# Grouped columns scaled and rotated one operation to a slot; gate tiles one to a block of the output projection

## What is computed

```
for l in range(2):
    sh_a, sc_a, g_a, sh_f, sc_f, g_f = split(silu(cond) @ w_ada[l] + b_ada[l], 6)   # 6 x 1024, for two cond
    z = modulate(x, norm_mix_g, sh_a, sc_a) @ w_in[l]      # 1824 columns: MLA, neighbourhood and grouped-query parts
    gq, gk = rms_norm(gq, q_g), rms_norm(gk, k_g)          # per head of 64, grouped-query columns
    o_gqa = attention(rope(gq), [rope(gk), cache], ...)    # latents rotated; 6 query heads, 2 key heads
    x += g_a * (concat(o_mla, o_na, o_gqa) @ w_out[l])     # 16 heads in all
    x += g_f * swiglu(modulate(x, norm_ffn_g, sh_f, sc_f)) # d_ff = 2816
```

## Time and profile before

| | us |
|---|---|
| median of 3 runs | 1801.14 |
| lowest and highest | 1798.12, 1805.73 |
| the profiled execution, its own time | 1804.04 |
| its span from first to last instruction | 1802.2 |
| PE busy in the span | 1708.5 |
| DVE, ACT, POOL busy | 1139.3, 691.9, 230.8 |

### The profile page before, as it was taken

How to read it: one execution, slowest core, us unless ns; L and a number is a source line. 1 busy time by engine, 2 the same in 40 slices (tenths; PEclk the granted TensorE clock), 3 DMA queues, 4 the chain that set the end, 5 groups by cost and what they waited for, 6 DMA issues and landing times.

```text
span 1802.2 us, 28539 instructions
## 1 busy us (share of the span) xinstructions
PE 1708.5 (95%) x11410; PEld 1636.7 (91%) x11410; DVE 1139.3 (63%) x2194; ACT 691.9 (38%) x1365; POOL 230.8 (13%) x318
## 2 busy tenths in 40 slices
PE   6998889989999999999999988988999999999997
PEld 2998778888999999999999977877999999999997
DVE  5997777848867766777562576785464444444443
ACT  3536657743422222222153476675352222222222
POOL 0134452300000000000011362331000000000001
PEclk8999999999999999999999999999999999999998
DMA  9552000045333333334132000003122222222201
GB/s 357 200 196 63 1 1 2 24 156 189 135 129 128 128 117 128 128 128 145 34 91 93 17 28 1 1 1 117 47 73 92 91 71 70 70 70 70 70 24 59
DMA packets 103206, 159.79 MB, mean 89 GB/s; under 512 B 4880, under 2 KB 81488, under 8 KB 102224
## 3 DMA queue, kind: packets, MB, share of 16 engines
q1 hardware_dynamic: 101632, 155.88, 25.6%
q0 software_dynamic: 480, 2.19, 0.4%
q10 hardware_dynamic: 1008, 0.61, 0.1%
HBM read 155.09 MB, written 3.57 MB: 88 GB/s over the span
## 4 chain that ended last, share of the span: by engine, by line
PE 84%; DVE 7%; ACT 3%; DMA 2%; issue 2%; POOL 1%; SPq 1%; POOLq 0%; DVEq 0%; ACTq 0%
PE ps L660 25%; PE ps L662 25%; PE ps L661 24%; PE ps L921 3%; PE ps L891 1%; DMA wo_raw<-in_w_out 1%; DVE ps L1410 1%; PE ps L893 1%; PE ps L668 1%; PE ps L740 1%; DMA ada_n<-in_w_ada_first 1%; DVE hT L1395 1%; DVE negmax L1646 1%; PE ps L796 1%; ACT probs L1196 1%
## 5 line engine op out<-in xcount | busy, mean ns | idle before, releaser
L660 PE MATMUL ps<-hT,gw 128*128 128x320 f32 x1408 | 435.2, 309 | 2.1 <-DVE hT L1395 2.1
L662 PE MATMUL ps<-hT,gw 128*128 128x320 f32 x1408 | 435.1, 309 | 0.0
L661 PE MATMUL ps<-hT,gw 128*128 128x320 f32 x1408 | 435.1, 309 | 0.0
L1478 DVE SCALAR_TENSOR_TENSOR x<-ps,mod,x 128x320 f32<-128x320 f32 (+2 forms) x576 | 211.8, 433 | 94.2 <-PE ps L662 91.1
L660 PEld LDWEIGHTS ps<-hT,gw 128*128 128x128 f32 x1408 | 264.4, 188 | 2.9 <-issue 2.9
L661 PEld LDWEIGHTS ps<-hT,gw 128*128 128x128 f32 x1408 | 264.4, 188 | 0.0
L662 PEld LDWEIGHTS ps<-hT,gw 128*128 128x128 f32 x1408 | 264.4, 188 | 0.0
L1728 DVE TENSOR_TENSOR mm<-sl,ps 128x320 f32<-128x320 f32 x88 | 42.7, 488 | 316.7 <-issue 185.3
L660 PE MATMUL ps<-act,dw 128*128 128x320 f32 x704 | 218.3, 310 | 2.7 <-DVE act L1395 2.7
L661 PE MATMUL ps<-act,dw 128*128 128x320 f32 x704 | 218.3, 310 | 0.0
L662 PE MATMUL ps<-act,dw 128*128 128x320 f32 x704 | 218.2, 310 | 0.0
(11 more groups left out here) (226 smaller groups left out, 3545.4 us busy)
## 6 DMA issues: line engine op xcount, KB each, us to landing
gw_raw<-in_w_gate SPq DMA_DIRECT2D x22, 1024.0 KB, 5.4
gw_raw<-in_w_up SPq DMA_DIRECT2D x22, 1024.0 KB, 8.0
dw_raw<-in_w_down SPq DMA_DIRECT2D x22, 1024.0 KB, 4.9
ada_w<-in_w_adaT SPq DMA_DIRECT2D x43, 512.0 KB, 5.7
ada_wf<-in_w_adaT SPq DMA_DIRECT2D x34, 512.0 KB, 7.0
wi_raw<-in_w_in SPq DMA_DIRECT2D x12, 1216.0 KB, 6.7
wo_raw<-in_w_out SPq DMA_DIRECT2D x16, 512.0 KB, 5.0
ada_n<-in_w_ada_first SPq DMA_DIRECT2D x5, 1024.0 KB, 15.6
```

The lines of the kernel that those rows point to most:

```text
L660: pe.matmul(dst, lh, rh, start=start, stop=False, skip_group_check=True)
L661: pe.matmul(dst, lh, rl, start=False, stop=False, skip_group_check=True)
L662: return pe.matmul(dst, ll, rh, start=False, stop=stop, skip_group_check=True)
L1478: i = ve.scalar_tensor_tensor(out=x[:, o, c0:c1], in0=ps[:, banks + hf_, s0:s0 + c1 - c0], scalar=mod[:, l, part * KD + o, q:q + 1], in1=x ...
```

## The change

It has three parts.

- **Grouped columns.** An entry ("GZ", t) becomes ("G1", t), the division, in slot 25 + 2t, ("G2", t), the gains, in slot 26 + 2t, both before the slot's transposition, and ("GR", t, j), the four POOL operations of the rotation, j = 0 to 3, in slots 28 + 4t + j. So tile 3's rotation is in slots 40 to 43, in both layers. The reciprocal of all tiles' roots (1581) stays with tile 0's division.
- **Gate tiles.** `GATE_AT` goes. Block 1 computes tile 40 ahead of its residual and tile 41 behind it, blocks 2 to 7 one tile each. ACT makes `silu_f` in block 1 instead of block 2. SP issues `silu_f` and tiles 40, 41 right at the end of attention and the first feed-forward weights only after `wo_raw[3]`, in both layers; then tiles 42 and 43, and one tile per block.
- **Layer 1's tiles in layer 0's feed-forward.** Block 0 computes its four behind its residuals, none ahead of the gated products. Other blocks stay.

```diff
-GATE_AT = [0, 0, 0, 0, 2, 4, 6, 7, 8]
...
-    spread([("GZ", t) for t in range(NT)], 25, 18)
+    for t in range(NT):
+        extra[2 * (25 + 2 * t)].append(("G1", t))
+        extra[2 * (26 + 2 * t)].append(("G2", t))
+    for t in range(4):
+        for j in range(4):
+            extra[2 * (28 + 4 * t + j)].append(("GR", t, j))
...
                     if o == 1:
 
                         sp.wait_ge(o_ready, l * 2 * NP + 2 * NP)
-                        sp.dma_start(gw_raw[:, 0], a["w_gate"][l, :, 0:256].rearrange("(k p) n -> p k n", p=P)).then_inc(gw_in, 16)
-                        sp.dma_start(gw_raw[:, 1], a["w_up"][l, :, 0:256].rearrange("(k p) n -> p k n", p=P)).then_inc(gw_in, 16)
-                        sp.dma_start(dw_raw[:], a["w_down"][l, 0:256, :].rearrange("(j p) n -> p j n", p=P)).then_inc(dw_in, 16)
                         if l + 1 < DEPTH:
...
-                    if l == 0 and o >= 2:
-                        for t in GATE[2:][GATE_AT[o - 1]:GATE_AT[o]]:
+                    if o == 3:
+                        sp.dma_start(gw_raw[:, 0], a["w_gate"][l, :, 0:256].rearrange("(k p) n -> p k n", p=P)).then_inc(gw_in, 16)
+                        sp.dma_start(gw_raw[:, 1], a["w_up"][l, :, 0:256].rearrange("(k p) n -> p k n", p=P)).then_inc(gw_in, 16)
+                        sp.dma_start(dw_raw[:], a["w_down"][l, 0:256, :].rearrange("(j p) n -> p j n", p=P)).then_inc(dw_in, 16)
+                    if l == 0 and o >= 3:
+                        for t in GATE[2:4] if o == 3 else GATE[o:o + 1]:
                             ada_load(l, t)
...
-                    if o == 2 and l + 1 < DEPTH:
+                    if o == 1 and l + 1 < DEPTH:
                         sc.wait_ge(cond_in, 32)
                         sc.activation(silu_f[:], silu_f[:], ACT.Silu).then_inc(silu_done, 1)
...
                     lo(wo[:, o % 2, 1], wo_raw[:, o % 2], wo[:, o % 2, 0]).then_inc(wo_ready, 1)
+                    if o == 1 and l == 0:
+                        ve.wait_ge(silu_done, 2)
+                        ada(l, GATE[0])
                     if o >= 1:
                         residual(l, l * XD + o, o - 1, 2 + 2 * ((o - 1) % 3), 2)
                     if o >= 4:
                         add_square(l, o - 3)
-                    if l == 0:
-                        if o == 3:
-                            ve.wait_ge(silu_done, 2)
-                        for t in GATE[GATE_AT[o]:GATE_AT[o + 1]]:
-                            ada(l, t)
+                    if o >= 1 and l == 0:
+                        ada(l, GATE[o])
...
-                        for t in ahead[2 * j:2 * j + 2]:
+                        for t in ahead[2 * j:2 * j + 2] if b else ():
                             ada(l + 1, t)
...
-                    for t in ahead[4:]:
+                    for t in ahead[4:] if b else ahead:
                         ada(l + 1, t)
```

More of the change, by code:

```diff
@@ L608, in _ @@
                 for s in SCHED:
-                    if s[0] == "GZ" and s[1] == NT - 1:
+                    if s == ("G2", NT - 1):
                         sp.wait_ge(g_norm, l * NT + NT)
@@ L1337, in _ @@
                         square(2 * l + 1, l * XD + 2, o - 3)
-                    if o == 2 and l + 1 < DEPTH:
+                    if o == 1 and l + 1 < DEPTH:
                         sc.wait_ge(cond_in, 32)
                         sc.activation(silu_f[:], silu_f[:], ACT.Silu).then_inc(silu_done, 1)
-                        sc.activation(warm[:, 0:1], eps[:], ACT.Sqrt)
+                        sc.activation(warm[:, 1:2], eps[:], ACT.Sqrt)
                 def gw_split(b, j):
@@ L1577, in g_scale, with g_divide @@
                 def g_scale(t):
+                    g_divide(t)
+                    g_gain(t)
+                def g_divide(t):
                     zg = z[:, t, OFF_G:G_V].rearrange("p (h d) -> p h d", h=8)
@@ L1678, in _ @@
                         i.then_inc(v_ready, 1)
-                    elif s[0] == "GZ" and l == 0:
-                        g_scale(s[1])
+                    elif s[0] == "G1" and l == 0:
+                        g_divide(s[1])
+                    elif s[0] == "G2" and l == 0:
+                        g_gain(s[1])
                 for o in range(KD):
@@ L1768, in _, with rotate_step @@
         def _(po):
-            def rotate(own, n, d, view, cos, sin, tmp):
+            def rotate_step(j, own, n, d, view, cos, sin, tmp):
                 w = d // 4
@@ L1774, in rotate @@
                 t4 = tmp.rearrange("p h (a b w) -> p h a b w", a=2, b=2)
-                for b in range(2):
-                    po.tensor_tensor(t4[:, :, :, b, :], halves[:, :, :, 1 - b, :],
-                                     s4[:, :, b, :].unsqueeze(1).broadcast_to([P, n, 2, w]), ALU.mult).then_inc(pool_own, 1)
-                po.wait_ge(pool_own, own + 2)
-                po.tensor_tensor(view, view, cos.unsqueeze(1).broadcast_to([P, n, d]), ALU.mult).then_inc(pool_own, 1)
+                if j < 2:
+                    return po.tensor_tensor(t4[:, :, :, j, :], halves[:, :, :, 1 - j, :],
+                                            s4[:, :, j, :].unsqueeze(1).broadcast_to([P, n, 2, w]), ALU.mult).then_inc(pool_own, 1)
+                if j == 2:
+                    po.wait_ge(pool_own, own + 2)
+                    return po.tensor_tensor(view, view, cos.unsqueeze(1).broadcast_to([P, n, d]), ALU.mult).then_inc(pool_own, 1)
                 po.wait_ge(pool_own, own + 3)
                 return po.tensor_tensor(view, view, tmp, ALU.add)
+            def rotate(*turn):
+                for j in range(4):
+                    i = rotate_step(j, *turn)
+                return i
             OWN = 3 * 12
@@ L1872, in _ @@
                         value_zeros(1)
-                    elif s[0] == "GZ" and (0 if l == 0 else LATE_G) <= s[1] < 4:
-                        g_rotate(s[1], ztmp[:])
+                    elif s[0] == "GR" and s[1] >= (0 if l == 0 else LATE_G):
+                        _, t, j = s
+                        if j == 0:
+                            po.wait_ge(g_norm, l * NT + t + 1)
+                            if t:
+                                po.wait_ge(g_roped, l * 4 + t)
+                        i = rotate_step(j, *g_turn(t, ztmp[:]))
+                        if j == 3:
+                            i.then_inc(g_roped, 1)
                 add_squares(l)
```

8 lines of the change are left out of this document (5 added, 3 removed).

## The result

The changed kernel takes 1788.88 us, the median of 9 runs (1787.45 to 1792.11), beside 1801.14 us for the kernel before (9 runs of the same comparison, 1794.8 to 1807.47): a ratio of 0.9938, 95% interval 0.9918 to 0.9958. The profiled execution took 1788.93 us with a span of 1787.1, against 1804.04 and 1802.2 before. In a second comparison the two gave 1788.26 (10 runs) and 1801.25 us (33 runs), ratio 0.9949, interval 0.9931 to 0.9968. The ratios are estimates of their own: the medians alone, divided, give 0.9932 and 0.9928.

What follows compares the result with a forecast made beforehand. PE was taken to bound the kernel nearly everywhere. Gains of 4.0 + 3.6 + 4.4 = 12.0 us take the profiled execution from 1804.0 to 1792 and the median from 1801.14 to 1789, range 1784 to 1796.

Steps and rivals of the forecast that it cites:

- Grouped columns, 4.0 predicted: Layer 0's attention, slots 25 to 47: 7.5 us lost before, 3.5 after, a gain of 4.0, bounds 5.9 and -1.8.
- the cost after: Attention, slots 25 to 47: 1.6 us lost on DVE plus 1.9 at the port, 3.5 in all.
- Its first item: Slot 25: reciprocal and division on DVE, 1.1 us, with no idle to cover them, 1.0 lost.
- The item for slots 28 to 34: DVE's gains and six further operations exceed its idle: 0.35 us lost in slot 28, 0.2 in slots 29 to 34.
- rival (b): Everything hidden: DVE's operations fall in its waits, one more clock window goes; 15.6 us gained, 1785.5; chance 0.14.
- The item for the port: Slots 28 to 34: seven meetings of DVE and POOL operations, a quarter of the 7.7 us bound, 1.9 lost.
- rival (a): Attention's port: seven meetings cost 1.1 us each, attention loses 9.3, total gain 6.2, 1795; chance 0.16.
- Gate tiles, 3.6 predicted: Output projection, blocks 1 to 6: earlier silu_f and one tile a block end PE's waits; 3.6 us gained, bound 0.
- rival (c): Projection: late silu_f delays tile 40, residual and block 2's split; block 2 starts 3 us late, 9.0 gained; chance 0.08.
- Feed-forward, 4.4 predicted: Block 0 without tiles takes 42.31 us, block 1's DVE idle covers the four moved; 4.4 gained, bounds 4.6 and 0.
- rival (e): Moved, not removed: the four tiles stall feed-forward block 1 as they did block 0; 7.6 us gained, 1793.5; chance 0.06.
- (d): Attention slower: ten slots can slip instead of five, 2.8 us a slot, 12.5 lost, 1814; chance 0.04.

Runs made afterwards that it cites:

- rotation_whole: The changed kernel with a tile's four POOL rotation operations in one slot again (28, 32, 36, 40); 1793.10 us (1 run).
- rotation_later: The changed kernel with the rotation behind the scaling, two operations to a slot in slots 35 to 42; 1787.71 us (1 run).
- both_later_earlier: The changed kernel with tile 47 behind the second norm's reciprocal and tile 0's reciprocal and division in slot 24; 1784.14 us (6 runs).
- weights_first: The changed kernel with the 3 MB of feed-forward weights issued ahead of silu_f and the gate tiles' loads again; 1788.96 us (1 run).
- first_scaling_earlier: The changed kernel with tile 0's reciprocal and division at the front of slot 24 instead of in slot 25; 1790.19 us (1 run).
- all_parts: The changed kernel itself, run beside its three parts on the same chip, against the kernel before; 1788.26 us (10 runs), ratio 0.9949.
- only_ffn: The kernel before with only the feed-forward part: block 0's four tiles moved to its end; 1799.35 us (12 runs), ratio 0.9993.

## Why the prediction held, point by point

**Grouped columns, 4.0 predicted, 6.3 measured.** The cost before (7.5) and its parts were right: of PE's lag, 1.7 us came in slot 25, 4.5 with the wait for a division and the 1.2 GHz behind it, and 1.2 later. rotation_whole brings back 4.7 us, 4.4 of them as one wait of 2.67 with one stretch at 1.2 GHz behind it. The term that was mis-sized is the cost after, 3.5 predicted, 1.2 measured. Its first item was right: slot 25, predicted 1.0, measured 1.02. The item for slots 28 to 34, 0.6, measured 0.2 (so the 5.9 us that I gave as the most to be won, with no meeting, was passed). So attention came out at 61.8 us, where the forecast had 64 and rival (b) 62.1: in this term the rival was nearer. The item for the port, 1.9, measured next to nothing on the path. DVE's operations did grow, by about as much as I gave them, but fewer of them, and two of the three beside a division of the probabilities and not beside a rotation. DVE and POOL of the changed kernel, in order of time:

```profile
238.69 1.23 DVE L1596 TENSOR_TENSOR z<-z,g 128x512 f32<-128x512 f32 x1
...
247.39 1.20 DVE L1592 TENSOR_TENSOR z<-z,stat 128x512 f32<-128x512 f32 x1
...
249.70 1.19 DVE L1596 TENSOR_TENSOR z<-z,g 128x512 f32<-128x512 f32 x1
...
238.07 1.31 POOL L535 TENSOR_SCALAR probs<-probs,rinv 128x640 f32<-128x640 f32 x1
...
247.30 0.74 POOL L1789 TENSOR_TENSOR ztmp<-z,rope 128x256 f32<-128x256 f32 x1
...
249.55 0.80 POOL L535 TENSOR_SCALAR probs<-probs,rinv 128x640 f32<-128x640 f32 x1 [1.51 <-DVE rinv L516]
```

Three of ten operations grew, by 0.54, 0.51 and 0.50, that is 1.6 us beside the 1.9 of the prediction. POOL paid more: its busy time in the stretch rose from 31.62 to 34.88 us with 38 instructions in both kernels, and nothing waited for it. The step that failed is the sum: it added every delay of DVE to the path, as if PE waited for each. DVE's lag went up to 2.30 us and came back to 1.18 in the slots behind, where DVE has waits, and PE's never went above 1.2. rotation_later, without any meeting of scaling and rotation, ends the same slots at the same 1.17. both_later_earlier, with three operations of 1.19 to 1.22 us in it, is 0.26 us behind layer 1 at slot 47. So the port's part of the cost is 0.3 us at most, and rival (a) falls. (Seven waits for a whole cosine product, 1.29 us each, would be 9.0, where the rival has 7.7; both are far above.) That layer 1's rows at 1.79 were a fair bound for one operation is right: rotation_whole has such a row, with POOL's beside it.

```profile
252.20 1.78 DVE L1592 TENSOR_TENSOR z<-z,stat 128x512 f32<-128x512 f32 x1
...
252.16 1.27 POOL L1795 TENSOR_TENSOR z<-z,ztmp 128x512 f32<-128x512 f32 x1
```

DVE's ends 0.55 us behind POOL's. The Trainium skill (SBUF — State Buffer, "Who interferes with whom") has the later of the two blocked for the other's whole instruction; this row agrees, the pair at the end of this document doesn't.

**Gate tiles, 3.6 predicted, 3.56 measured,** by the chain as given. DVE has 5.1 us of work in a block, 5.4 predicted. Counted back from the first residual, `silu_f` was forecast 7.2 us ahead and came 8.5 ahead (368.9 and 377.4), and tile 40 was done 4.0 ahead instead of 1.2. weights_first shows that rival (c) named a real mechanism, with 4.3 us as its price. What I did not list is the load of tile 42 behind the 3 MB: I looked at the wait for tile 41 and at `wo_raw[4]`, and first_scaling_earlier shows the load itself 2.48 us late, at 0.6 us of cost.

**Feed-forward, 4.4 predicted, 4.46 measured,** block 1 unchanged as said, rival (e) refuted in all_parts and only_ffn alike.

**The sum, 12.0 predicted, 14.3 in the stretches, 15.1 in the span, 12.3 in the medians.** Two differences nearly cancel: the stretches gave 2.3 us more than forecast, and the medians fell by 2.0 less than the stretches. The prediction took the second difference as nil, since it subtracted the same 12.0 from the median. So that 1789 and 1788.88 agree within 0.2 us is luck; the mechanism stands on the three stretches. The interval of the second comparison, 5.8 to 12.4 us, doesn't reach their 14.3. By the medians less the stretches, the rest is 1.3 us longer in the changed kernel there (an estimate: 160.6 us of stretches and 1.8 outside the span off 1801.25, 146.4 and 1.8 off 1788.26), and why is open. The scatter of the rest, 1636.5 to 1642.4 over fourteen traces, is larger than any single term here but the first.

**Rivals (b) and (d).** (b), everything hidden, would have been a cost after of 1.6 us with one more stretch at half clock gone. The stretch's own cost, 1.2, is even below that; the time is not, since the rest lost nothing of the kind: it is the same within 1 to 2 us. (d) needed 1.55 us a slot; the changed kernel pays 1.2 in all slots together.

## What to carry to other kernels

Before a cost is added to the path, set the stretch beside one that lacks the work and follow the lag of the engine that bounds it, here PE: a helper's delay can be made up in its own waits before that engine asks for it, and one that has nothing to cover it (slot 25 here) isn't made up. In rotation_whole an operation too long for its slot did its harm at the one place where something short and urgent was queued behind it; splitting it there alone was not tried. And judge an edit worth 1 to 4 us of 1800 in its own stretch, between the same two instructions: the totals of single executions differed by up to 6 us for reasons outside every edit.
